# Two transformer blocks in float32: the feed-forwards' tiles turned by transposing DMAs instead of on TensorE

## What is computed

```
# first block
h = rmsnorm(x, norm_ffn)
x = x + (silu(h @ w_gate) * (h @ w_up)) @ w_down
# second block
h2 = rmsnorm_2(x, norm2_g)
u = causal_dwconv(einsum('bsd,df->bsf', h2, w_up), conv_w, conv_b)   # out[t] = sum_j w[j] * u[t-2+j] + b, 3 taps
u_gate, u_val = u[..., :5632], u[..., 5632:]
x = x + einsum('bsf,fd->bsd', silu(u_gate) * u_val, w_down)
```

## Time and profile before

| | |
|---|---|
| median of 3 runs | 2542.66 us (2542.53 to 2543.4) |
| the profiled execution's own time | 2542.45 us |
| its span, first to last instruction | 2540.7 us |
| busy: PE, PEld, DVE, ACT, POOL | 2533.9, 2099.3, 1413.6, 1229.0, 138.8 us |
| DMA queue q1 (SP's): bytes, share of 16 engines | 467.30 MB, 61.3% |

### The profile page before, as it was taken

One profiled execution on the slowest core, in us unless ns is written; L12 is line 12 of the kernel. 1 busy time (PEld: TensorE's weight loads), 2 busy tenths in 40 slices (PEclk: granted clock), 3 DMA queues, 4 the chain that ended last, 5 costly groups with the idle time before them and its releaser, 6 DMA issues.

```text
span 2540.7 us, 33424 instructions
## 1 busy us (share of the span) xinstructions
PE 2533.9 (100%) x11596; PEld 2099.3 (83%) x11596; DVE 1413.6 (56%) x1707; ACT 1229.0 (48%) x1698; POOL 138.8 (5%) x211
## 2 busy tenths in 40 slices
PE   9999999999999999999999999999999999999999
PEld 7888888888888888888888888888888888888887
DVE  5555555555555555555455555565566646665665
ACT  6555445444344434455444544544555445553553
POOL 2222200000000000000000111100000000000000
PEclk9999999999999999999999999999999999999999
DMA  8555556665666566666666666655666566666665
GB/s 239 161 171 161 169 173 185 191 189 189 193 190 189 190 192 190 191 198 190 179 185 179 182 185 179 184 176 189 184 182 190 190 192 187 178 193 195 184 189 166
DMA packets 327827, 471.16 MB, mean 185 GB/s; under 512 B 23232, under 2 KB 126244, under 8 KB 327584
## 3 DMA queue, kind: packets, MB, share of 16 engines
q1 hardware_dynamic: 326352, 467.30, 61.3%
q0 software_dynamic: 1088, 2.07, 0.3%
q10 hardware_dynamic: 272, 0.26, 0.0%
HBM read 467.44 MB, written 2.11 MB: 185 GB/s over the span
## 4 chain that ended last, share of the span: by engine, by line
PE 99%; DMA 0%; SPq 0%; DVE 0%; ACT 0%; issue 0%
PE ps L473 32%; PE ps L475 32%; PE ps L474 31%; PE ps L922 1%; PE ps L722 1%; PE ps L567 0%; PE ps L549 0%; PE ps L582 0%; PE ps L555 0%; PE ps L756 0%; PE ps L639 0%; PE ps L659 0%; PE ps L888 0%; DMA raw<-in_w_in 0%; PE ps L592 0%; PE ps L863 0%
## 5 line engine op out<-in xcount | busy, mean ns | idle before, releaser
L1395 DVE TENSOR_TENSOR w_lo<-raw,w_hi 128x1024 fp32r<-128x1024 f32 x880 | 1081.1, 1230 | 1078.6 <-ACT w_hi L976 1076.5
L976 ACT ACTIVATE w_hi<-raw 128x1024 fp32r<-128x1024 f32 x880 | 931.3, 1060 | 1182.3 <-PE ps L475 1172.9
L473 PE MATMUL ps<-w_hi,xT_hi 128*128 128x512 f32 x2204 | 873.3, 396 | 0.5 <-DVE xT_lo L1414 0.5
L475 PE MATMUL ps<-w_hi,xT_lo 128*128 128x512 f32 x2204 | 859.8, 390 | 0.0
L474 PE MATMUL ps<-w_lo,xT_hi 128*128 128x512 f32 x2204 | 858.3, 389 | 0.0
L473 PE MATMUL ps<-w_hi,yT_hi 128*128 128x512 f32 x1312 | 515.2, 393 | 0.0
L475 PE MATMUL ps<-w_hi,yT_lo 128*128 128x512 f32 x1312 | 511.2, 390 | 0.0
L474 PE MATMUL ps<-w_lo,yT_hi 128*128 128x512 f32 x1312 | 510.6, 389 | 0.0
L475 PEld LDWEIGHTS ps<-w_hi,xT_lo 128*128 128x128 f32 x2204 | 413.7, 188 | 87.2
L473 PEld LDWEIGHTS ps<-w_hi,xT_hi 128*128 128x128 f32 x2204 | 414.0, 188 | 85.9 <-issue 2.7
L474 PEld LDWEIGHTS ps<-w_lo,xT_hi 128*128 128x128 f32 x2204 | 414.2, 188 | 82.9
(11 more groups left out here) (204 smaller groups left out, 899.7 us busy)
## 6 DMA issues: line engine op xcount, KB each, us to landing
raw<-in_w_up SPq DMA_DIRECT2D x264, 512.0 KB, 3.7
raw<-in_w_down SPq DMA_DIRECT2D x176, 512.0 KB, 3.8
raw<-in_w_in SPq DMA_DIRECT2D x160, 512.0 KB, 3.8
raw<-in_w_gate SPq DMA_DIRECT2D x88, 512.0 KB, 3.7
raw<-in_w_out SPq DMA_DIRECT2D x60, 512.0 KB, 3.7
raw<-in_w_in SPq DMA_DIRECT2D x128, 192.0 KB, 2.8
raw<-in_w_in SPq DMA_DIRECT2D x192, 128.0 KB, 2.5
raw<-in_w_proj_m SPq DMA_DIRECT2D x16, 512.0 KB, 3.8
```

The lines of the kernel that those rows point to most:

```text
L473: pe.matmul(o, hi[:, q], w_hi[n % NS][:, k, 0:width], start=first, stop=False)
L475: mm = pe.matmul(o, lo[:, q], w_hi[n % NS][:, k, 0:width], start=False, stop=last)
L976: nc.scalar.activation(w_hi[n % NS][:, :, 0:width], raw[n % NS][:, :, 0:width], ACT.Copy).then_inc(hi_ready, 1)
L1395: v.tensor_tensor(w_lo[n % NS][:, :, 0:width], raw[n % NS][:, :, 0:width], f32(w_hi[n % NS][:, :, 0:width]), ALU.subtract).then_inc(lo_rea ...
```

## The change

- The 8 transposes on PE of every turn go, 33 turns in all (11 of `turn_act`, 22 of `turn_u`).
- GpSimd copies each token tile of the values into `halves`, the low and the high 16 bits of each number apart (`halve`, two copies a turn).
- SP issues a transposing DMA for each token tile into `flipped` (two a turn), right behind its load of unit e + 8, where e is the last unit of the group (`SENT`, `AHEAD`), and waits before each for the halving (`halved`). SP's loops over units are written out.
- GpSimd waits for both (`across`) and puts the 16-bit halves together again in `turned` (`join`, two copies a turn), behind a wait for the readers of the tile before.
- ACT and DVE read `turned` in SBUF instead of PSUM, one unit later than before: behind unit 3 in the first feed-forward, and behind units 10 to 13 (gate half) and 2 to 4 (up half) in the second.
- `prob`, `mix`, `pT`, `y` and `stage` move into one tile `work`, which the new buffers share with them. The turns of the residual rows (`turn_x`) stay on PE.

```diff
+def turns():
+    es = [PH[f"ffn1_up{t}"][0] + 16 * i + 15 for t in range(3) for i in range(THIRDS[t] // W)] + [PH[f"ffn2_up{t}"][0] + 16 * i + 8 * g + 7 for t in range(3) for i in range(THIRDS[t] // W) for g in range(2)]
+    return {e: k for k, e in enumerate(es)}
...
+        halves = work[:, 0:4 * S].bitcast(U16).rearrange("p (t e n) -> p t e n", t=NT, e=2)
+        flipped = work[:, 4 * S:8 * S].bitcast(U16).rearrange("p (e f s) -> p e f s", e=2, s=S)
+        turned = work[:, 8 * S:12 * S].rearrange("p (f s) -> p f s", s=S)
+        turned_halves = work[:, 8 * S:12 * S].bitcast(U16).rearrange("p (n e) -> p n e", e=2)
...
                 sp.dma_start(raw[n % NS][:, :, 0:width], src).then_inc(raw_landed[n % NS], 16)
+                if n + i * step - AHEAD in SENT:
+                    k = SENT[n + i * step - AHEAD]
+                    for t in range(NT):
+                        sp.wait_ge(halved, 2 * k + t + 1)
+                        sp.dma_start_transpose(flipped[:, :, :, t * P:(t + 1) * P].rearrange("p e f s -> p (e f) s"),
+                                               halves[:, t, :, :].rearrange("p e n -> p (e n)")).then_inc(across, 16)
...
-                with sp.Fori(0, loops) as i:
+                for i in range(loops):
...
                     with pe.Fori(1, n_fg) as i:
-                        def behind(u):
-                            if u == 0:
-                                turn_u(1, fg0 - 1, i)
-                            if u == 8:
-                                turn_u(0, fg0, i)
-                        up_turn(i, behind)
+                        up_turn(i, nothing)
...
-                            if u == 2:
+                            if u == 3:
                                 hi_part(fg0 - 1, i)
...
-                        if u == 9:
+                        if u == 10:
                             first_tap(i, 0, gate_z)
...
                     def late(u, i):
 
-                        if u in (1, 2):
-                            up_half(i, u - 1)
                         if u in (2, 3):
-                            act_lo_part(i, u - 2)
+                            up_half(i, u - 2)
+                        if u in (3, 4):
+                            act_lo_part(i, u - 3)
...
+            def halve(z, t):
+
+                g_.tensor_copy(halves[:, t, :, :], z[:, t, :].bitcast(U16).rearrange("p (n e) -> p e n", e=2)).then_inc(halved, 1)
+
+            def join(b):
+
+                c = slice(b * 2 * S, (b + 1) * 2 * S)
+                return g_.tensor_copy(turned_halves[:, c, :], flipped.rearrange("p e f s -> p (f s) e")[:, c, :])
+
+            def landed(i, k, step=0):
+                pool.wait_ge(across, at(i, 32 * (k + 1), 32 * step))
...
+                    for g in range(2):
+                        for tt in range(NT):
+                            pool.wait_ge(by_act, at(i, FREE + PH[f"ffn2_up{t}"][BY_ACT] + 2 * g + tt + 1, 4))
+                            halve(tok_u[g], tt)
+                        landed(i, TURNS["ffn2"] + 2 * fg0 + g, 2)
+                        pool.wait_ge(conv_step, at(i, 16 * fg0 + 8 * g, 16))
+                        join(0)
+                        join(1).then_inc(tok_u_T[g], 1)
```

More of the change, by code:

```diff
@@ L25 @@
 X = mybir.AxisListType.X
+U16 = mybir.dt.uint16
 P = 128
@@ L113, with done @@
 FREE = 3
+def done(early, units, g):
+    return 2 * EARLY + (g + 1) * (units - EARLY) - 1 if early else (g + 1) * units - 1
+AHEAD = 2 * NS
+def turns():
+    es = [PH[f"ffn1_up{t}"][0] + 16 * i + 15 for t in range(3) for i in range(THIRDS[t] // W)] + [PH[f"ffn2_up{t}"][0] + 16 * i + 8 * g + 7 for t in range(3) for i in range(THIRDS[t] // W) for g in range(2)]
+    return {e: k for k, e in enumerate(es)}
 def loads_of(n):
@@ L136, in evacuated @@
     return FREE + PH[name][1] + 2 * (3 * (head // 4) + groups[head % 4])
+TURNS, turns_ = {}, 0
+for name_, n_ in (("ffn1", 11), ("ffn2", 22),):
+    TURNS[name_], turns_ = turns_, turns_ + n_
 def at(i, c, step):
     return c if i is None else i * step + c
+SENT = turns()
 class Head:
@@ L787, in ffn1 @@
                     if t == 2:
-                        residual(down, units, yT, 0, 2 * KT, ready=act_ready, first=first, early=True)
+                        residual(down, units, yT, 0, 2 * KT, ready=act_ready, early=True)
                     else:
@@ L791, in ffn1 @@
                             for g in range(2):
-                                group(down, i, 2 * units, g, units, yT, 0, evac_free(by_dve, down, BY_DVE, i, g), ready=act_ready,
-                                      behind=first if i == 0 else nothing)
+                                group(down, i, 2 * units, g, units, yT, 0, evac_free(by_dve, down, BY_DVE, i, g), ready=act_ready)
                     fg0 += n_fg
@@ L957, in ffn2 @@
                         if t == 2 and i == 0:
-                            early_groups(down, units, xT, None, act_ready, first)
+                            early_groups(down, units, xT, None, act_ready, nothing)
                             continue
@@ L961, in ffn2 @@
                             group(down, i, 2 * units, g, units, xT, 0, evac_free(by_dve, down, BY_DVE, i, g), ready=act_ready,
-                                  behind=first if i == 0 else nothing, halves=t == 2 and i == 1 and g == 1)
+                                  halves=t == 2 and i == 1 and g == 1)
                     fg0 += n_fg
@@ L1168, in hi_part @@
                         for b in range(2):
-                            nc.scalar.activation(yT_hi[:, ds(at(i, (2 * b - 4) * S, 4 * S), 2 * S)], ps[4 + b][:], ACT.Copy).then_inc(tok_hi, 1)
+                            c = ds(at(i, (2 * b - 4) * S, 4 * S), 2 * S)
+                            nc.scalar.activation(yT_hi[:, c].rearrange("p (f s) -> p f s", s=S), turned[:, 2 * b:2 * b + 2, :], ACT.Copy).then_inc(tok_hi, 1)
                     def behind(u):
@@ L1335, in first_tap @@
                             col = at(i, 4 * fg0 + f + g * (CONV_T // 2), 4)
-                            nc.scalar.activation(z[:, f, :], ps[4 + 2 * g + f // 2][:, f % 2 * S:(f % 2 + 1) * S], ACT.Identity,
+                            nc.scalar.activation(z[:, f, :], turned[:, f, :], ACT.Identity,
                                                  scale=conv[:, ds(col + 2 * CONV_T, 1)], bias=conv[:, ds(col + 3 * CONV_T, 1)]).then_inc(conv_start, 1)
@@ L2002, in _ @@
             g_.tensor_tensor(half_r_sq[:], rstd[:], half_r[:], ALU.mult).then_inc(ffn_scale, 1)
+            fg0 = 0
+            for t, width in enumerate(THIRDS):
+                for i in range(width // W):
+                    for tt in range(NT):
+                        pool.wait_ge(by_dve, at(i, FREE + PH[f"ffn1_up{t}"][BY_DVE] + 3 + tt, 4))
+                        halve(tok_act, tt)
+                    landed(i, TURNS["ffn1"] + fg0, 1)
+                    pool.wait_ge(tok_lo, at(i, FREE + 2 * fg0, 2))
+                    join(0)
+                    join(1).then_inc(tok_T, 1)
+                fg0 += width // W
             keep("ffn1_down2")
@@ L2047, in _ @@
             factor(5, rstd).then_inc(rstd_ready, 1)
+            pool.wait_ge(kt_lo, 5 * KT)
+            fg0 = 0
+            for t, width in enumerate(THIRDS):
+                for i in range(width // W):
+                    for g in range(2):
+                        for tt in range(NT):
+                            pool.wait_ge(by_act, at(i, FREE + PH[f"ffn2_up{t}"][BY_ACT] + 2 * g + tt + 1, 4))
+                            halve(tok_u[g], tt)
+                        landed(i, TURNS["ffn2"] + 2 * fg0 + g, 2)
+                        pool.wait_ge(conv_step, at(i, 16 * fg0 + 8 * g, 16))
+                        join(0)
+                        join(1).then_inc(tok_u_T[g], 1)
+                fg0 += width // W
 _INS = ['x', 'norm_attn', 'w_in', 'lambda_qk', 'subln', 'w_out', 'norm_ffn', 'w_gate', 'w_up', 'w_down', 'norm_final',
```

68 lines of the change are left out of this document (19 added, 49 removed).

## The result

| | before | after |
|---|---|---|
| median of the runs | 2542.69 us (2542.5 to 2543.4, 6 runs) | 2549.57 us (2548.7 to 2552.05, 6 runs) |
| ratio to before | | 1.0029, 95% interval 1.002 to 1.0039 |
| profiled execution, its span | 2542.45 us, 2540.7 us | 2549.74 us, 2547.9 us |

The 33 turns are gone from TensorE (PE), which should have given 30.4 us; instead 7.3 us were added in the profiled execution, so 37.7 us went into something new.

The account below looks back on a forecast made before the run. TensorE's own work was taken to bound the kernel. Removing 33 turns (-30.4 us) and adding waits of 6.6 and 1.8 gave -22.0, so 2520 us forecast; own range 2512 to 2535, with rivals 2512 to 2614.

Parts of the forecast that it names:

- what bounds the kernel: Whole kernel: TensorE, busy 2533.9 of 2540.7 us at its higher clock; other engines cost time only where it waits.
- the turn's price: Between two units on TensorE: a turn costs 0.92 us, so removing 33 saves 30.4 us.
- the chain of one turn, up to the tile: Second feed-forward: copy out of PSUM, halvings, transposes, joins; halved by +4.4, landed at +9.6, tile ready at +12.6 us.
- The join: GpSimd's copy putting 16-bit halves together: 1.04 us each, upper bound 2.8; an estimated 1.56 by the Trainium skill.
- The transposing DMA: SP's 256 KB transposes: 5.1 us to land, lower end 2.2, small pieces up to 23.6 us.
- rival (b): Transposing DMAs are slow, one behind the other: with 5.1 us more, 102 us of waits, 2614 us; chance 0.20.
- Covered, with 1.1 us to spare: Second feed-forward, up half: DVE's second weight split ends at +20.7, TensorE wants it at +21.8 us, so no wait.
- SP's queue: Weight loads behind SP's wait for GpSimd: SP free at +4.9, next load due +5.1, 7.2 us of slack, no cost.
- if ACT's splits wait for raw, it is SP's queue instead: Sign to look for: ACT's splits waiting for loaded weights would mean SP's queue is at fault; no size given.
- the down-projections: Behind the first and second third, second feed-forward: TensorE waits 3.3 us at unit 6, twice, 6.6 us in all.
- the first feed-forward: Tile ready at +14.8: up groups in time, unit 6 behind two thirds 0.9 us late, 1.8 us in all.
- Rival (a): Turned tile too late, with joins of 2.8 us: waits of 44 us against 30.4, 2556 us; chance 0.31.

Follow-up runs that it names:

- ffn1_only: Against the kernel before: only the first feed-forward is turned by DMA, the second stays as it was; 2532.7 us, ratio 0.9961.
- the best version: Against the changed kernel: up-half readers one unit later, transposes issued one weight load earlier, all three down-projections in the early order; 2513.61 us (0.9884 to the kernel before).
- gates_and_ffn1: Against the changed kernel: the 11 up halves of the second feed-forward are turned by TensorE again, readers at their old units; 2523.22 us (0.9924 to before).
- no_transposes: The changed kernel without its transposing DMAs; the joins read a constant block, so values are wrong; 2514.42 us (0.9888 to the kernel before).
- no_copies: The changed kernel without its 132 GpSimd copies; SP transposes a constant block into the readers' tile, so values are wrong; 2514.37 us (0.9888 to before).
- last_pe: Against the changed kernel: the last up half ahead of each down-projection (3 of 33 turns) is turned by TensorE; 2535.22 us (0.9971 to before).
- early_down: Against the changed kernel: up-half readers two units later, all three down-projections in the early order, all 33 turns by DMA; 2519.57 us (0.9907 to before).
- one_load_later: Against the changed kernel: SP issues the transposes one weight load later; 2600.16 us (1.0229 to the kernel before).

## Why the prediction was wrong

**Right: what bounds the kernel, and the turn's price.** 0.92 us a turn on PE: taking 11 turns off it (ffn1_only) measured 9.9 us against 10.1, 22 turns 19.3 against 20.2, and the best version 29.1 of 30.4.

**Right: the chain of one turn, up to the tile.** Ready at +12.6 in a gate half that stands alone, as the sum had it. The join, my largest doubt, was no trouble: 1159 ns in the median of the 66, 11% over the 1.04 us taken. The Trainium skill (GPSIMD Engine Reference, Performance pitfalls for Q7 kernels) led to an estimate of 1.56 us; the trace disagrees, for a plain copy whose step is 2 KB. The transposing DMA landed in 4.8 us in the median against 5.1 taken; the estimate of 10.5 us from the Trainium skill (VectorE: DVE Perf Modes, The three transpose paths) did not come true. What the Trainium skill says in Advanced Engine Details and Errata (X-Bar Transpose), that transposing DMAs are as fast as others, is nearer to these rows: weight loads of twice the bytes landed in 4.1 to 4.4 us. So rival (b) was not what happened.

**Wrong: "Covered, with 1.1 us to spare".** This is the step that failed, and the forecast's sign with it. It priced one turn as if the engines came to it rested. In the changed kernel ACT and DVE reach the up half's readers before the tile and stand there; the sum had them wait as well and called it covered, since no PE wait followed from that turn. But what they then make up for lies on the next turn 21.8 us later: the copies out of PSUM end 0.4 us later, the halvings 1.5 us, the transposes' landing 2.5, the first tap 2.7. The second split behind it ends 1.7 us past its due time where 1.1 were to spare. Of the 2.7 us at the first tap 1.8 are the tile's lateness; the other 0.9 are the step from the tile to DVE's first tap, a term of the sum that was too small (0.6 us where a turn alone measured 1.5, +12.6 to +14.1). With that term right the sum would have left 0.2 us to spare. gates_and_ffn1 (turns 43.5 us apart, no burst), no_transposes and no_copies (chain short enough) show the lateness from three sides.

**Wrong: "SP's queue".** I asked whether the weight loads would suffer behind SP's wait, and they hardly did. The other direction decided: what the load issued just ahead does to the transposes, by holding SP until +5.1 and by being still under way when they are issued. With one load fewer ahead of them it is 26 us less. I had even named the sign ("if ACT's splits wait for raw, it is SP's queue instead"; they wait 28.4 us), but for the wrong victim.

**Mis-sized: the down-projections.** 3.3 us twice forecast, 5.8 and 6.4 measured (12.2 in sum): the first tap's lateness (2.7 us) added in full. The forecast had no term for the clock behind such waits. last_pe prices both at 17.1 us where the sum had 6.6.

**Mis-sized, the harmless way: the first feed-forward.** 1.8 us of waiting forecast, none measured; with ACT's waits of at most 0.8 us for GpSimd, its 11 turns save all.

**Rival (a) happened, with another cause.** Its effect (PE waits for w_lo and in the down-projections, in the second halves) and its sensitivity were right: it decided at "about 2.5 us later" and gave 2556 for 3.5 us; measured were 1.8 us at the tile and 2.7 at the first tap, and 2549.6. Its cause, slow joins, is refuted by the 1.16 us.

## What to carry to other kernels

When work leaves the bound engine for a longer chain through others, price two turns in a row, not one: a reader that stands waiting catches up in a burst, and the burst lands on the chain's next round. Ask of a DMA in a shared queue not only whom it delays but what stands ahead of it at that moment and whether that has landed; its place there was worth more (26 us) than either one or two units of extra room for its readers. And add the lower clock to each wait of the bound engine of a few microseconds.

## What the runs showed of the hardware

- A transposing DMA of 128 x 1024 two-byte elements from SBUF to SBUF: issue 1.24 us on SP in the median, landing 3.1 us at least. Where a 512 KB weight load had been issued 0.4 us ahead of a turn's first one, the turn's second held SP for up to 3.97 us, and the slowest landed after 7.5 us. From ScalarE's queue 8.2 us in the median.
- A one-input GpSimd copy of 1024 elements takes 1.04 us alone and 1.9 to 2.0 us while DVE's splits run back to back; where it started beside a single split, DVE's split was the one that grew, from 1.23 to 1.47 us.
- Reading the turned tile from SBUF rather than PSUM did not shorten the readers: ACT's first taps took 590 ns in the mean against 557 in the kernel before.
- The granted clock fell to 0.50, its lower level, behind waits of TensorE of 5.8 and 6.4 us, but also of 2.6 us (early_down) and 2.2 us (kernel after), and not behind another of 2.6 us (one_load_later, 1909.65). A fall cost about 2 to 3 us, as much as the shorter waits themselves.
